# Per-head sums of squares on Trainium2: one fp32 product replaced by two products of rounded operands

## What is computed

```python
proj = jnp.einsum('bsd,dc->bsc', hn, w_in)
qkv_a, z, beta_raw, alpha_raw, qkv_b, gates = jnp.split(proj, SPLIT_POINTS, axis=-1)
qkv_a = jax.nn.silu(centred_depthwise_conv(qkv_a, conv_w))
qa, ka, va = [t.reshape(bn, s, A_HEADS, A_HEAD_DIM) for t in jnp.split(qkv_a, 3, axis=-1)]
qa, ka = l2norm(qa), l2norm(ka)

def l2norm(x):
    xf = x.astype(jnp.float32)
    return xf * lax.rsqrt(jnp.sum(xf * xf, axis=-1, keepdims=True) + EPS)
```

## Time and profile before

| | before |
|---|---|
| median of three runs | 2506.6 us |
| lowest and highest | 2499.77, 2509.13 us |
| profiled execution, own time | 2499.77 us |
| profiled execution, span from first to last instruction | 2499.7 us |
| TensorE busy | 2366.1 us, 95% |
| VectorE busy | 1389.4 us, 56% |
| ScalarE busy | 1078.9 us, 43% |
| POOL busy | 396.2 us, 16% |
| mean granted TensorE clock | 0.981 |

### The profile page before, as it was taken

One profiled execution on the slowest core, in us unless ns is written; L12 is line 12 of the kernel. 1 busy time (PEld: TensorE's weight loads), 2 busy tenths in 40 slices (PEclk: granted clock), 3 DMA queues, 4 the chain that ended last, 5 costly groups with the idle time before them and its releaser, 6 DMA issues. The chain is left out here.

```text
span 2499.7 us, 49530 instructions
## 1 busy us (share of the span) xinstructions
PE 2366.1 (95%) x20758; PEld 2111.5 (84%) x20758; DVE 1389.4 (56%) x1772; ACT 1078.9 (43%) x1601; POOL 396.2 (16%) x411
## 2 busy tenths in 40 slices
PE   7999999999999999888988999899999999999996
PEld 5777888999999888888964555599999999999996
DVE  6555311244545276333345448777777777777775
ACT  4666310011111176111145553266666666666664
POOL 1000000000000175654433110000010000100001
PEclk9999999999999999999999999999999999999998
DMA  3333422168566466644454432467778777777765
GB/s 121 89 88 106 140 82 107 70 177 265 185 201 185 151 195 197 210 127 132 123 175 145 146 120 71 182 262 258 262 257 285 271 243 277 260 269 256 268 225 200
DMA packets 174171, 461.27 MB, mean 185 GB/s; under 512 B 57360, under 2 KB 103056, under 8 KB 146352
## 3 DMA queue, kind: packets, MB, share of 16 engines
q1 hardware_dynamic: 160944, 412.63, 49.3%
q0 software_dynamic: 13024, 45.70, 6.4%
HBM read 359.94 MB, written 102.24 MB: 185 GB/s over the span
## 5 line engine op out<-in xcount | busy, mean ns | idle before, releaser
L78 DVE TENSOR_TENSOR ex_w_rest<-weights,ex_w_rounded 128x2048 fp32r<-128x2048 f32 x192 | 439.5, 2290 | 204.4 <-ACT ex_w_rounded L2724 202.5
L2724 ACT CAST ex_w_rounded<-weights 128x2048 fp32r<-128x2048 f32 x192 | 365.6, 1905 | 12.3 <-PEq L48 12.3
L2616 PE MATMUL ex_g_acc<-ex_xt,ex_w_rounded 128*128 128x320 f32 x1024 | 270.3, 347 | 2.1 <-ACT ex_xt L2736 2.1
L2616 PE MATMUL ex_u_acc<-ex_xt,ex_w_rounded 128*128 128x320 f32 x1024 | 271.7, 348 | 0.0
L2617 PE MATMUL ex_u_acc<-ex_xt,ex_w_rest 128*128 128x160 f32 x1024 | 242.1, 236 | 0.0
L2617 PE MATMUL ex_g_acc<-ex_xt,ex_w_rest 128*128 128x160 f32 x1024 | 242.1, 236 | 0.0
L2617 PEld LDWEIGHTS ex_g_acc<-ex_xt,ex_w_rest 128*128 128x128 f32 x1024 | 196.4, 192 | 0.0
L2617 PEld LDWEIGHTS ex_u_acc<-ex_xt,ex_w_rest 128*128 128x128 f32 x1024 | 196.4, 192 | 0.0
L2616 PEld LDWEIGHTS ex_g_acc<-ex_xt,ex_w_rounded 128*128 128x128 f32 x1024 | 193.0, 188 | 2.5 <-issue 2.5
L2616 PEld LDWEIGHTS ex_u_acc<-ex_xt,ex_w_rounded 128*128 128x128 f32 x1024 | 193.1, 189 | 0.2
L85 PE MATMUL ch_wide<-normed,ch_w_rounded 128*128 128x512 f32 x384 | 154.1, 401 | 2.9 <-PEq L48 2.2
(11 more groups left out here) (423 smaller groups left out, 5577.9 us busy)
## 6 DMA issues: line engine op xcount, KB each, us to landing
weights<-in_w_expert SPq DMA_DIRECT2D x192, 1024.0 KB, 5.0
laq<-sc_laq SPq DMA_DIRECT2D x20, 768.0 KB, 3.5
dl_la<-laq SPq DMA_DIRECT2D x20, 768.0 KB, 5.1
tk_w<-in_w_tok SPq DMA_DIRECT2D x10, 1344.0 KB, 6.4
ch_w<-in_w_ch SPq DMA_DIRECT2D x24, 512.0 KB, 5.5
sc_rows<-rows SPq DMA_DIRECT2D x40, 256.0 KB, 6.3
sc_qk<-qkv_ch SPq DMA_DIRECT2D x40, 256.0 KB, 6.2
dl_kv<-qkv_tok SPq DMA_DIRECT2D x40, 256.0 KB, 5.1
```

The costliest lines, as they stand in the source:

```text
L78: return dve.tensor_tensor(out, whole, rounded.bitcast(F32), ALU.subtract)
L2616: pe.matmul(bank[:, 0:2 * SLOTS], hi[:, cols], x.rearrange("p a n -> p (a n)"), start=first, stop=False, skip_group_check=True)
L2724: act.copy(w_hi[:, i % SPLIT], held[:, i % HELD]).then_inc(w_rounded, 1)
```

## The change

The squares are no longer one fp32 matrix but two matrices of rounded values (`F32R`). ScalarE's Square writes its result rounded (`sq_hi`). POOL computes the same square again, whole (`ch_sq`), and then subtracts the rounded one from it (`sq_lo`). TensorE multiplies both by a rounded copy of the head matrix, that ScalarE makes once, and adds the two in PSUM. `sq_hi` and `sq_lo` lie in the buffers of the next phase's first weights, so VectorE's last steps of the phase wait for the last head sum. POOL's store of a tile's token rows is now queued behind the squares of the tile two further on.

```diff
+        headsum_r = sb("ch_headsum_rounded", [P, P], F32R)
+        sq_hi = tokens.rounded.rearrange("p k c -> p (k c)")[:, 0:GAP]
+        sq_lo = tokens.rest.rearrange("p k c -> p (k c)")[:, 0:GAP]
...
-                def store(c, b, i):
+                def store(c, b):
                     pool.wait_ge(tok_done, 3 * c + 3)
                     pool.dma_start(dr["qkv_tok"][:, bass.ds(c * P, P)].rearrange("(t p) c -> p t c", p=P), tok[:, b]).then_inc(tok_out[b], 16)
-                walk(pool, A_TILES, 0, store)
+
+                def squares(c, b, i):
+                    pool.wait_ge(silu_done, c + 1)
+                    pool.tensor_tensor(sq[:], act_out[:, b], act_out[:, b], ALU.mult).then_inc(sq_whole, 1)
+                    pool.wait_ge(sq_whole, c + 1)
+                    pool.wait_ge(sq_done, c + 1)
+                    if not early(c, 1):
+                        pool.wait_ge(ss_done, c)
+                    pool.tensor_tensor(sq_lo, sq[:], sq_hi.bitcast(F32), ALU.subtract).then_inc(sq_rest, 1)
+                    if not early(c, 2):
+                        store(c - 2, b)
+                walk(pool, A_TILES, 2, squares)
+                for c in range(A_TILES - 2, A_TILES):
+                    store(c, c % 2)
...
                 def head_sums(c, b):
                     if early(c, 1):
-                        pe.wait_ge(const_ready, 48)
-                    pe.wait_ge(sq_done, c + 1)
+                        pe.wait_ge(sum_rounded, 1)
+                    pe.wait_ge(sq_rest, c + 1)
...
-                        mm = pe.matmul(aux[:, j, 0:n], headsum[:], sq[:, at:at + n], start=True, stop=True)
+                        pe.matmul(aux[:, j, 0:n], headsum_r[:], sq_hi[:, at:at + n], start=True, stop=False)
+                        mm = pe.matmul(aux[:, j, 0:n], headsum_r[:], sq_lo[:, at:at + n], start=False, stop=True)
                     mm.then_inc(ss_done, 1)
...
                 act.wait_ge(const_ready, 48)
+                act.copy(headsum_r[:], headsum[:]).then_inc(sum_rounded, 1)
...
                     if not early(c, 2):
                         act.wait_ge(kn_done, c - 1)
+                    if not early(c, 2):
+                        act.wait_ge(sq_whole, c - 1)
                     act.activation(act_out[:, b], conv[:], ACT.Silu).then_inc(silu_done, 1)
...
-                    act.activation(sq[:], act_out[:, b], ACT.Square).then_inc(sq_done, 1)
+                    act.activation(sq_hi, act_out[:, b], ACT.Square).then_inc(sq_done, 1)
...
                 dve.wait_ge(tokens.loaded, 16)
+                dve.wait_ge(ss_done, A_TILES)
                 dve.tensor_copy(tokens.rounded[:], tokens.whole[:]).then_inc(tokens.rounded_done, 1)
```

More of the change, by code:

```diff
@@ L278, in phase_channels @@
         sq_done = sem("ch_sq_done")
+        sum_rounded = sem("ch_headsum_rounded_done")
+        sq_whole, sq_rest = sem("ch_sq_whole_done"), sem("ch_sq_rest_done")
         ss_done = sem("ch_ss_done")
```

## The result

The changed kernel takes 2555.9 us in the median of four runs (2554.65 to 2560.25), the kernel before 2503.2 us in the median of its four (2499.45 to 2509.13; the fourth run is new). The ratio is 1.0224, with a 95% interval of 1.0203 to 1.0245: slower by 53 us in the medians, 56 us by the ratio. The profiled execution has a span of 2553.3 us and a time of 2554.98 us.

The account below looks back on a forecast made before the run. A ring through silu, squares, head sums and logarithm sets the pace in twelve tiles. Its stretch grows 2.90 us plus 1.0 for the low clock, 3.9 per tile, 47 for twelve: 2553 us median, range 2528 to 2582.

Parts of the forecast that it names:

- What bounds the kernel: First twelve tiles: a ring of waits between engines sets the pace, 18.55 us per tile; TensorE has slack.
- the ring: Per tile: taps, silu, squares, head sums, logarithm, exponential, copy of chunk 2, next taps; each link waits for the one ahead.
- the mean stretch: From silu's end to the logarithm's start: 3.81 us before, 6.71 after without the clock term, 2.90 longer per tile.
- POOL's two instructions: Product 2.31 and difference 2.88 us ahead of the head sums, together 5.19, bounds 4.62 to 7.22.
- rival C: VectorE and POOL block each other: if VectorE's cast came first, up to 1.9 us per tile, 2576 us; 6%.
- The head sums and the clock: Rounded sums cost 1.36 us; TensorE's 4.8 us idle stretch brings the clock to 1.2 GHz, adding 1.0 per tile.
- chunk 2 hides its own slow part: Chunk 2 behind the sums slows partly, but has 1.3 us of slack against the exponential; nothing charged.
- The handovers: Silu to POOL, POOL to itself, POOL to TensorE: three waits, 0.16 us per tile together.
- The sum: Profiled execution 2499.8 + 47 = 2547 us; 2553 us for the median.
- Rival D: Not slower: a pair no longer than ScalarE's 1.28 us square shortens the ring 1.01 us, 12 in all, 2494; 5%.
- The store of the token rows: POOL's store, queued behind the difference, lands 6.7 us after issue, still hidden with 3.9 us to spare.

Follow-up runs that it names:

- the split held back: Changed kernel, but VectorE's split of the next weights also waits until POOL's difference is done: 2549.8 us, ratio 1.0212.
- the two runs that came closest: Changed kernel with TensorE not awaiting POOL: sums from rounded squares alone, no POOL work, 2506.0 us; POOL's pair kept, rounded squares multiplied twice, 2499.0 us.
- these moves: Changed kernel: head sums after chunk 2, chunk 2 copied before the logarithm, VectorE's multiplication after three taps, weights issued one turn earlier: 2493.1 us, ratio 0.9980.
- the moves by themselves, with fp32 sums: Kernel before, no POOL work: head sums after chunk 2, chunk 2 copied before the logarithm, weights issued one turn earlier: 2495.9 us, ratio 0.9986.
- the fp32 sums behind the pair: Changed kernel, TensorE still waiting for both POOL instructions, but three fp32 products of POOL's whole squares as sums: 2578.4 us, ratio 1.0291.
- the run with 20 extra matmuls: Changed kernel with 20 extra 128-column matmuls per tile on TensorE ahead of its wait for POOL: 2546.8 us, ratio 1.0183.

## Why the prediction was right, and where it was off

Forecast 2553 us with a range of 2528 to 2582; measured 2555.9. Part of the closeness is luck: the forecast stood on a median of three of 2506.6. With the fourth run it is 2503.2, from where the same sum gives 2550. What was worked out is the difference, 47 us for the profiled execution, and that was 53.6.

**What bounds the kernel: right.** The loss followed the ring from silu to the logarithm and came back in each tile: 8.31 - 3.88 = 4.43 us in the mean stretch, 4.51 in the distance of tiles. The run that kept POOL's work and dropped the wait shows that it is the wait.

**POOL's two instructions: right for the product, short for the difference.** I took 2.31 and 2.88 us, and measured 2.32 and 3.31. The line through the row of a square and the row of a sum of two tiles held to the hundredth, as 2.88 is what the difference takes when VectorE is quiet; the rounded output cost nothing. The term that failed is in rival C, where I called the blocking hidden because POOL would hold the port first. It does for the product. But I had placed the cast 4.6 us after silu, as in the one tile of the earlier trace rows; in the changed kernel the weights land earlier in the tile, and in the last eleven tiles the cast is issued 1.0 to 2.2 us after silu ends, while the product runs. It waits for the product's end and is then served ahead of the difference, which takes 0.43 us longer for it. I had priced the case in which VectorE comes first at up to 1.9 us; it was 0.43, since only the rest of the cast stands in the way, and the subtraction comes behind the difference. As I said, VectorE's own delay (3.88 against 1.23 us) costs nothing. The Trainium skill, SBUF — State Buffer, section SBUF: two separate sides, has the port pair as an exclusive lock for the whole instruction; by that rule the trace agrees, with 3.31 against 2.88 us and 3.88 against 1.22 us for the split held back. "Starts first" has to be read as the moment of issue: the cast, issued at 203.20 while the product ran, went ahead of the difference, issued at 203.71.

**The head sums and the clock: right.** TensorE's idle stretch was 3.8 to 5.1 us where I had 4.8 (the profile's brackets count 0.17 us less than I did, 0.57 against 0.74 in the earlier trace rows), and a fall of the clock came with every one of the twelve. The sums took 2.54 us in eleven tiles, where I had 1.36 + 1.0 = 2.36; in the first the clock fell only behind them, and they took 1.44. Keeping TensorE busy took 1.07 us off them, so the term and its cause are shown. That chunk 2 hides its own slow part is right too: ScalarE copies it at once after the exponential.

**The handovers: short.** 0.16 us was 0.21 to 0.32.

**The sum.** Difference +0.43, sums +0.18, handovers +0.05 to +0.16, and -0.07 because the stretch before was 3.88 us in the mean and not the 3.81 of one tile: some 0.6 on top of 3.9 us a tile, 4.5. Twelve times 0.6 is the 7 us that were missing. So the mechanism held, and the term that was most short is POOL's difference.

**Rival D: its price was wrong.** For a pair no longer than ScalarE's square I expected 12 us of gain, and 20 and 13 in the two runs that came closest. Those runs gained nothing and 3 us in the medians (ratios 1.0009 and 0.9984), with tiles 0.4 us closer in both. The stretch has a floor of 3.09 us in ScalarE's own queue. It was to be read in the earlier trace rows: the logarithm waits 0.73 us, so a faster head sum could gain at most that much, 9 us over twelve tiles, before the weights take their part.

**The rest.** The store of the token rows hid with more to spare than expected: it landed 4.4 us after its issue instead of 6.7, and ScalarE never waited for it. Nothing after the stage moved by more than the executions differ.

## What to carry to other kernels

A cheaper instruction in a ring is a gain only if its inputs do not come later by more than it saves: find the ring that sets the pace, and count the new producer (here 5.6 us of POOL for 1.28 us of ScalarE) before the saving (1.0 us of TensorE). What an engine waits in a ring is also the most that its releaser can give back, so look for the second-longest arm before promising a gain. And when a step must wait for a slow engine, move it behind work that is independent of it, and check which loads were queued behind what you moved: with these moves the same POOL work went from 53 us of loss to 8 us under the kernel before, and the moves by themselves, with fp32 sums, gave 5. The gain is that of the moves; of the change it is only shown that it then costs nothing clear of the noise.

## What the runs showed of the hardware

- An elementwise POOL instruction and VectorE's cast and subtraction block each other in whole instructions: the subtraction of 128x1024 took 3.88 us beside POOL and 1.22 without, the cast up to 1.98 and 0.69. A cast issued while POOL's product ran was served ahead of POOL's difference, which took 3.31 us instead of 2.88.
- POOL's difference with a rounded result took 2.88 us for 1282 columns, what the row of a sum of two fp32 tiles foretold; POOL's product of a tile with itself took 2.32, a fifth less for the same number of columns.
- At a granted 0.5 an fp32 product slows as a rounded one does: 2.45 to as much as 4.67 us for the three.
- Idle stretches of TensorE of about 2 us, repeated in each tile, were also followed by falls of the clock, in seven tiles of the run with POOL's pair and the sums moved behind chunk 2; one fall for every tile came with stretches of 3.4 us and more (the changed kernel, the fp32 sums behind the pair, the split held back), and none with stretches of about 0.6 us and less (the run with 20 extra matmuls, and POOL's pair with the weights issued earlier, but for 1.0 us in its first tile).
